# Two stacked transformer models on one core: what each block does to hand its result to the next one

## The chip, the cores and the metric

The kernel runs on one core of a Trainium2 chip. The metric is the device time of one execution in microseconds (us), lower is better. All arithmetic is float32; matrix products of weights and activations are done as three products of reduced float32 parts, explained below.

## The reference, cut to what matters

256 tokens of width 1024 go through two models one after the other. The first has two equal layers; each computes a modulated root-mean-square norm of the running sum `x`, a mixer (sparse and compressed attention of two kinds), and adds a gated, normalized result. The second has four sublayers: neighbourhood attention, a gated feed-forward net, latent attention, and a mixture of eight experts.

```python
# first model, per layer l
h = rmsnorm(x, g_pre[l]) * (1.0 + scale) + shift
y = hybrid_mixer(h, ...)
x = x + gate * rmsnorm(y, g_post[l])
# second model, per sublayer; rmsnorm without a weight
h = _rmsnorm(x) * (1 + sc[:, None, :]) + sh[:, None, :]
m = attention(h)            # or feed-forward, or experts
x = x + g[:, None, :] * m
```

`scale`, `shift` and `gate` come from products of one conditioning vector with large matrices (here called "ada" sums); they don't depend on `x`. What matters here is the seam between two of these blocks: nothing of the next block's products can begin before its `h` is there, `h` needs the mean square of a whole row of `x`, and `x` needs the whole last product of the block before.

## The kernel before, in words

**Layout.** `x` is held as two halves of 128 token rows (m = 0 and m = 1) with 1024 columns each. The products need features on the partitions, so `h` is kept turned, in 8 tiles of 128 features by 256 tokens (`hb`, and its two parts `h_hi` and `h_lo`). Every float32 operand is split into a high part (ScalarE, ACT, copies it with rounding) and a low part (VectorE, DVE, subtracts), and one product is three matmuls (`mm3`, L831 to L835): hi*hi, hi*lo, lo*hi.

**Weights.** All weights come as steps of 128x2048 elements (1 MB) through a ring of 6 raw buffers, loaded by SyncE's queue (L681) as soon as a buffer is free. For a weight step ACT writes `w_hi` (`hi_to`, L1625) and DVE writes `w_lo` (`raw_to`/`split_to`, L2217) into a ring of 3 split buffers; TensorE (PE) frees a split buffer with `split_used`. For an "ada" step DVE does eight scaled sums (L2233, L2235) instead. A projection slot of PE is two weight steps, kh = 0 and kh = 1; kh = 0 uses feature tiles 0 to 3, kh = 1 tiles 4 to 7. There are 48 matmuls of 256 columns in one half slot of `feat_pieces` (L869).

**Order.** Each engine has one queue, written out by hand and executed in order; semaphores tie them. Phases are `lay0`, `lay1`, `na`, `ffn`, `mla` and then routing and experts.

**A seam (lay0 to lay1 as the example).** PE's last product `out_moba(1)` (L1038) ends. ACT squares and sums the output rows (L1960), GpSimd (POOL) turns the sum into 1/rms in two instructions, the mean (L734) and the power (L739), DVE scales the output by the gate (L2728) and adds it to `x` (L2731), for m = 0 early and for m = 1 last. Then `squares` (L1633): ACT squares all of `x`, m = 0 and m = 1; POOL `rstd` (L729) makes both 1/rms at once; meanwhile DVE makes `w_lo` of the next block's first weight step and the per-feature factors `ab` (`make_ab`, L2291); then `normed` (L2253) writes `xn` = x/rms, both halves, and only then PE turns it: `turn` (L913) does 16 transposes, four for each of four PSUM banks (a bank holds two feature tiles of 256 tokens), and signals `turned` after each bank. ACT and DVE scale and shift the turned tiles (`scaled`, banks 0 and 2 on DVE, 1 and 3 on ACT), ACT writes `h_hi`, DVE `h_lo` (`lo` in `norm`, L2261), each signal `h` meaning one pair of feature tiles. DVE's order is scaled(0), lo(0), scaled(2), lo(1), lo(2), lo(3). PE's first slot waits for `h` 2 before kh = 0 and for `h` 4 before kh = 1; in `ffn` PE waits for `h` 4 before everything. After `norm` DVE goes on to `w_lo` of the second weight step (in lay1 it first multiplies gate and g_post, L2521, 1.23 us).

In the feed-forward block `x` is updated by `update_x` (L2306) after the last product of both row halves, in eight DVE instructions of 512 columns (L2313, L2314); PE's last work there is the 24 matmuls of `down(10)` over both row halves, then `ada(11)`. In `na` the update is L2800 and L2802, in `ffn` and `na` without a second norm. POOL also fills `nakz` with zeros in `na` (L760 and L762), waiting for `xn` and for `turned`.

```python
            def turn(src):
                for b in range(4):
                    for k in range(2):
                        for m in range(MT):
                            ...
                    last.then_inc(*e.inc("turned"))
```

Of the kernel before, what the change touches and what calls it, by code (L numbers as in the profile page):

```python
# [12 lines left out]
P = 128  # L13
# [152 lines left out]
def ring_plan(size, lengths):  # L166
# [78 lines left out]
    "dve": {"pre": 26, "lay0": 93, "lay1": 81, "na": 46, "ffn": 104, "mla": 29, "rt": 10, "go": 23, "moe0": 11, "moeA": 7, "moeB": 7, "moeZ": 7, "more": 7},  # L245
# [47 lines left out]
    "rstd": {"lay": 3, "na": 1, "ffn": 1, "mla": 3, "rt": 2, "end": 1},  # L293
# [6 lines left out]
    "sq": {"lay": 4, "na": 2, "ffn": 2, "mla": 6, "rt": 2, "end": 2},  # L300
# [9 lines left out]
    "x_half": {"mla": 1},  # L310
# [82 lines left out]
def build(nc, dram):  # L393
    ctx = ExitStack()
    with ctx:
# [326 lines left out]
        def _(pool):  # L722
# [6 lines left out]
            def rstd(sq_wait, spans):  # L729

                pool.wait_ge(*e.at("sq", sq_wait))
                pool.sem_inc(settled)
                for a, b, n in spans:
                    g.tensor_scalar(st[:, s_ms + a:s_ms + b], st[:, s_sq + a:s_sq + b],  # L734
                                    1.0 / n, EPS, ALU.mult, ALU.add).then_inc(*e.inc("mean_sq"))
                    pool.wait_ge(*e.last("mean_sq"))
                    pool.sem_inc(settled)
                a, b = spans[0][0], spans[-1][1]
                g.tensor_tensor(st[:, s_rs + a:s_rs + b], st[:, s_ms + a:s_ms + b],  # L739
                                st[:, s_half:s_half + b - a], ALU.pow).then_inc(*e.inc("rstd"))  # L740
# [10 lines left out]
            for l in range(2):  # L751
                e.enter(f"lay{l}")
                rstd(2, [(0, 2, D)])
                rstd(3, [(2, 3, D)])
                rstd(4, [(3, 4, D)])
            e.enter("na")
            rstd(2, [(0, 2, D)])
# [69 lines left out]
        def _(pe):  # L827
# [22 lines left out]
            def tok_pieces(n, banks, width, first=True, fresh=False):  # L850

                for kh in range(2):
                    w = arrived(n + kh)
                    if fresh:
                        pe.wait_ge(*e.at("h", 2 * kh + 2))
                    for m in range(MT):
                        if kh == 0 and first:
                            bank_free(banks[m])
                        for k in range(4):
                            kt = kh * 4 + k  # L860
                            lhs = [a[:, kt, m * P:(m + 1) * P] for a in (hh, hl)]
                            rhs = [a[:, k * width:(k + 1) * width] for a in w]
                            last = mm3(PS[:, banks[m], 0:width], lhs, rhs, kt == 0, kt == KT - 1)
                            if m == MT - 1 and k == 3:
                                last.then_inc(*e.inc("split_used"))
                            if k % 2 == 1:
                                yield

            def feat_pieces(n, banks, order=(0, 1, 2, 3), fresh=False):  # L869

                for kh in range(2):
                    w = arrived(n + kh)
                    if fresh:
                        pe.wait_ge(*e.at("h", 2 * kh + 2))
                    for i, f in enumerate(order):
                        b = banks[i // 2]
                        if kh == 0 and i % 2 == 0:
                            bank_free(b)
                        for k in range(4):
                            kt = kh * 4 + k  # L880
# [2342 lines left out]
```

## Time and profile before

| what | value |
|---|---|
| median of 3 runs | 1628.31 us (1627.68 to 1629.74) |
| the profiled execution, its own time | 1633.32 us |
| its span in the trace | 1631.4 us |
| PE / DVE / ACT / POOL busy | 87% / 75% / 53% / 4% |
| DMA, mean over the span | 247 GB/s |
| mean granted TensorE clock | 0.94 |

The page's parts are: busy time of each engine over the span, the same in 40 slices with the granted clock, DMA queues, the chain that ended last, the costliest groups by line. The timeline lists instructions by start time and length, with the engine's idle time before one, and what ended it, in brackets. A row with "x2" is several merged neighbours: start of the first, busy time of all.

### The profile page before, as it was taken

What the parts mean: (1) busy time and instruction counts of PE and PEld (TensorE: products, weight loads), DVE (VectorE), ACT (ScalarE), POOL (GpSimd) and SP (SyncE); (2) the same over time, 40 slices, a digit from 0 to 9 for tenths busy, and PEclk for the clock granted to TensorE, in tenths of its full rate; (3) what the DMA queues carried; (4) which work ended last, traced back from release to release, by engine and by line L of the source; (5) the groups of instructions that cost most, each with busy time, mean ns of one, the idle gap of its engine ahead of it and who ended that gap; (6) DMA issues with size and microseconds to landing.
All of it is one profiled execution on the core that took longest, in us unless ns stands there. A gap on an engine that the chain in (4) does not pass through costs nothing.

```text
span 1631.4 us, 21240 instructions
## 1 busy us (share of the span) xinstructions
PE 1414.9 (87%) x7628; PEld 1188.4 (73%) x7628; DVE 1216.6 (75%) x1484; ACT 861.2 (53%) x1210; POOL 65.3 (4%) x82
## 2 busy tenths in 40 slices
PE   2999878899979896899985896999999999999992
PEld 2878668787668775898964785877777777777772
DVE  7978646776485647788767535889889889899895
ACT  2434444345344534334414645677777777777772
POOL 1000000000010000000001004000000000000001
PEclk9989998899889998999987996999999999999996
DMA  9945415555165724677753214889999999999782
GB/s 398 369 173 212 173 60 197 197 209 203 52 237 217 269 78 154 253 276 290 297 201 125 102 61 153 315 335 364 355 349 355 338 353 364 342 366 362 281 361 90
DMA packets 61537, 403.08 MB, mean 247 GB/s; under 512 B 6534, under 2 KB 9734, under 8 KB 15116
## 3 DMA queue, kind: packets, MB, share of 16 engines
q1 hardware_dynamic: 52416, 379.45, 61.4%
q10 hardware_dynamic: 7020, 15.17, 2.6%
q0 software_dynamic: 2016, 7.34, 1.2%
q8 instruction: 52, 0.85, 0.2%
q14 instruction: 33, 0.27, 0.0%
HBM read 393.01 MB, written 8.91 MB: 246 GB/s over the span
## 4 chain that ended last, share of the span: by engine, by line
PE 49%; DVE 33%; ACT 10%; issue 4%; DMA 3%; POOL 1%; ACTq 0%; DVEq 0%; SPq 0%; POOLq 0%
DVE w_lo L2217 18%; PE PS L833 13%; PE PS L835 12%; PE PS L834 12%; DVE acc L2235 4%; ACT w_hi L1625 4%; DMA raw<-in_ws 2%; ACT xg L1720 2%; PE PS L986 1%; PE PS L903 1%; PE PS L1006 1%; DVE a_lo L2384 1%; PE PS L995 1%; DVE hb L2393 1%; DVE hb L2395 1%
## 5 line engine op out<-in xcount | busy, mean ns | idle before, releaser
L2217 DVE TENSOR_TENSOR w_lo<-raw,w_hi 128x2048 fp32r<-128x2048 f32 x287 | 659.6, 2298 | 150.7 <-ACT w_hi L1625 127.9
L1625 ACT ACTIVATE w_hi<-raw 128x2048 fp32r<-128x2048 f32 x287 | 548.0, 1919 | 246.0 <-PE PS L835 221.9
L833 PE MATMUL PS<-w_hi,h_hi 128*128 128x512 f32 (+2 forms) x812 | 337.3, 415 | 26.2 <-DVE h_lo L2660 8.3
L835 PE MATMUL PS<-w_hi,h_lo 128*128 128x512 f32 (+2 forms) x812 | 320.1, 394 | 0.0
L834 PE MATMUL PS<-w_lo,h_hi 128*128 128x512 f32 (+2 forms) x812 | 319.5, 393 | 0.0
L833 PE MATMUL PS<-h_hi,w_hi 128*128 128x256 f32 x776 | 234.5, 302 | 33.4 <-DVE h_lo L2268 14.4
L834 PE MATMUL PS<-h_lo,w_hi 128*128 128x256 f32 x776 | 226.8, 292 | 0.0
L835 PE MATMUL PS<-h_hi,w_lo 128*128 128x256 f32 x776 | 226.6, 292 | 0.0
L833 PEld LDWEIGHTS PS<-w_hi,h_hi 128*128 128x128 f32 x812 | 156.8, 193 | 74.4 <-DVE w_lo L2217 16.0
L2235 DVE SCALAR_TENSOR_TENSOR acc<-raw,cs,acc 128x512 f32<-128x512 f32 x252 | 189.5, 752 | 9.0
L833 PEld LDWEIGHTS PS<-h_hi,w_hi 128*128 128x128 f32 x776 | 156.2, 201 | 38.5 <-issue 11.6
L835 PEld LDWEIGHTS PS<-w_hi,h_lo 128*128 128x128 f32 x812 | 156.2, 192 | 33.1
L834 PEld LDWEIGHTS PS<-w_lo,h_hi 128*128 128x128 f32 x812 | 157.1, 193 | 29.0 <-issue 2.2
L834 PEld LDWEIGHTS PS<-h_lo,w_hi 128*128 128x128 f32 x776 | 156.2, 201 | 2.4 <-issue 1.7
L835 PEld LDWEIGHTS PS<-h_hi,w_lo 128*128 128x128 f32 x776 | 155.9, 201 | 0.0
L833 PE MATMUL PS<-w_hi,a_hi 128*128 128x512 f32 x340 | 140.0, 412 | 17.3 <-DVE a_lo L2384 11.1
L835 PE MATMUL PS<-w_hi,a_lo 128*128 128x512 f32 x340 | 134.4, 395 | 0.0
L834 PE MATMUL PS<-w_lo,a_hi 128*128 128x512 f32 x340 | 133.7, 393 | 0.0
L1886 ACT ACTIVATE lgp<-lgp,st 128x128 f32<-128x128 f32 (+1 forms) x96 | 42.9, 449 | 123.9 <-DVE st L2536 123.9
L833 PEld LDWEIGHTS PS<-w_hi,a_hi 128*128 128x128 f32 x340 | 64.4, 190 | 37.6 <-DVE w_lo L2217 23.1
L835 PEld LDWEIGHTS PS<-w_hi,a_lo 128*128 128x128 f32 x340 | 64.4, 189 | 14.6
L834 PEld LDWEIGHTS PS<-w_lo,a_hi 128*128 128x128 f32 x340 | 64.6, 190 | 11.9
(310 smaller groups left out, 1397.9 us busy)
## 6 DMA issues: line engine op xcount, KB each, us to landing
raw<-in_ws SPq DMA_DIRECT2D x359, 1024.0 KB, 5.5
y_rows<-ysb ACTq DMA_DIRECT2D x10, 512.0 KB, 7.2
rp<-in_rp ACTq DMA_DIRECT2D x8, 384.0 KB, 4.8
ckb<-in_ck ACTq DMA_DIRECT2D x2, 1024.0 KB, 6.5
y_rows<-ones ACTq DMA_DIRECT2D x3, 512.0 KB, 8.2
x<-in_x SPq DMA_DIRECT2D x1, 1024.0 KB, 13.4
gpost<-in_gpost ACTq DMA_DIRECT2D x2, 512.0 KB, 5.7
x_rows<-xn_f ACTq DMA_DIRECT2D x2, 512.0 KB, 3.8
```

Of the source, the lines that this page charges most:

```text
L833: t.matmul(out, lhs[0], rhs[0], start=start, stop=False, skip_group_check=True)
L834: t.matmul(out, lhs[0], rhs[1], start=False, stop=False, skip_group_check=True)
L835: return t.matmul(out, lhs[1], rhs[0], start=False, stop=stop, skip_group_check=True)
L903: last = t.matmul(PS[:, 3, c:c + 1], a[:, c * P:(c + 1) * P], ones[:, 0:1], start=True, stop=True)
L986: t.matmul(PS[:, PS_S[i % 2], 0:2 * u["nk"]].rearrange("p (a k) -> p a k", a=2), u["q"], u["k"], start=True, stop=True).then_inc(*e.inc("s ...
L995: last = t.transpose(PS[:, PS_PT, c * P:(c + 1) * P], lgp[:, i % 3, c * P:(c + 1) * P], ident)
L1006: last = t.matmul(PS[:, PS_O, h * HD:(h + 1) * HD], ptp[:, i % 2, (a * n + c) * P:(a * n + c + 1) * P], u["v"][a][c], start=c == 0, stop=c ...
L1625: a.activation(wh[:, SPL_AT[e.phase][i], :], raw[:, r, :], ACT.Copy).then_inc(*e.inc("hi"))
L1720: ins = a.activation(xg[:, kt, :], PS[:, 6 + kt // 4, (kt % 4) * P:(kt % 4 + 1) * P], ACT.Identity, scale=ab[:, 0, kt:kt + 1], bias=ab[:, ...
L1886: a.activation(part, part, ACT.Exp, bias=mn(c), scale=-1.0, accum_out=sm(c)).then_inc(*e.inc("probs"))
L2217: v.tensor_tensor(wl[:, s, :], raw[:, r, :], wh[:, s, :].bitcast(F32), ALU.subtract).then_inc(*e.inc("raw_used"))
L2235: ins = v.scalar_tensor_tensor(out=dst, in0=w, scalar=c[:, kt:kt + 1], in1=dst, op0=ALU.mult, op1=ALU.add)
```

## The change

At each of the four seams lay0 to lay1, lay1 to na, na to ffn and ffn to mla, the first 128 rows go ahead. As soon as x of m = 0 is updated, ACT squares it (after `w_hi` of the next block's first step), POOL makes its 1/rms, DVE makes `w_lo` of that step and writes xn of m = 0 (`hand_on`), and PE transposes it (8 transposes, or 4 in mla, where two banks are still in use) before xn of m = 1 is there. For m = 1 the squares are taken in two halves of 512 columns, each with its own sum; POOL takes the mean of the first sum, and adds the second with one more instruction. x of m = 1 is updated by column halves. After xn of m = 1 PE needs 2 transposes for a bank, instead of 4.

DVE's order in `norm` becomes scaled(0), lo(0), lo(1), scaled(2), lo(2), lo(3), and the first slot of a block runs over feature tiles 0 and 1, then 2 and 3 (and 4 and 5, then 6 and 7), waiting for one `h` more each time; in ffn the wait for `h` 4 goes. In lay0 (no seam ahead of it) POOL's work and the waits are split in the same way, and the order of `norm` and of the first slot changes too. In ffn the last down product does the m = 0 rows first, then `ada(11)`, then m = 1 by column halves. ACT makes `w_hi` of the third step after `h_hi`, and not before it.

```diff
+            def rstd_halves(col, other, sums, done, name):
+                pool.wait_ge(*e.at(sums, 2))
+                pool.sem_inc(settled)
+                mean(col, col + 1, D, name)
+                pool.wait_ge(*e.at(sums, 3))
+                pool.sem_inc(settled)
+                g.tensor_scalar(st[:, s_ms + other:s_ms + other + 1], st[:, s_sq + other:s_sq + other + 1],
+                                1.0 / D, st[:, s_ms + col:s_ms + col + 1], ALU.mult,
+                                ALU.add).then_inc(*e.inc(name))
+                ...
+                g.tensor_tensor(... ALU.pow).then_inc(*e.inc(done))
...
+            for block, following in (("lay0", "lay1"), ("lay1", "na")):
+                e.resume(block)
+                rstd(1, [(2, 3, D)])
+                e.enter(following)
+                rstd(1, [(0, 1, D)], "sq_x", "rstd_x", "mean_x")
+                e.resume(block)
+                rstd_halves(3, 7, "sq", "rstd", "mean_sq")
+                e.resume(following)
+                rstd_halves(1, 6, "sq_x", "rstd_x", "mean_x")
...
             def feat_pieces(n, banks, order=(0, 1, 2, 3), fresh=False):
                 for kh in range(2):
                     w = arrived(n + kh)
-                    if fresh:
-                        pe.wait_ge(*e.at("h", 2 * kh + 2))
-                    for i, f in enumerate(order):
+                    for ks in ((0, 1), (2, 3)) if fresh else ((0, 1, 2, 3),):
+                        if fresh:
+                            pe.wait_ge(*e.at("h", 2 * kh + ks[-1] // 2 + 1))
+                        for i, f in enumerate(order):
...
+            def turn(src, banks_free=4):
+                ...
+                pe.wait_ge(*e.at("xn", 1))
+                for b in range(banks_free):
+                    part(b, 0)
+                pe.wait_ge(*e.at("xn", 2))
                 for b in range(4):
+                    if b >= banks_free:
+                        part(b, 0)
+                    part(b, 1).then_inc(*e.inc("turned"))
...
+                    order = ([(k, m, c) for k in range(2) for m in range(MT) for c in range(2)] if not ends else
+                             [(k, 0, c) for k in range(2) for c in range(2)] +
+                             [(k, 1, c) for c in range(2) for k in range(2)])
+                        if ends and (k, m, c) == (1, 0, 1):
+                            last.then_inc(*e.inc("out_m0"))
+                            ada(FFN_SLOTS)
...
-            pe.wait_ge(*e.at("h", 4))
             ffn()
...
+            def squares_on(xn):
+                for half in range(2):
+                    square(xn, 1, half)
+                hi_to(2)
...
+                following, xn = (("lay1", xn_l), ("na", xn_n))[l]
+                start(following)
+                square(xn, 0)
+                e.resume(f"lay{l}")
+                for c, col in enumerate((3, 7)):
+                    act.wait_ge(*e.at("split_used", 19 + c))
+                    a.activation(xn_l[:, 1, c * 512:(c + 1) * 512], PS[:, PS_OUT[1] + c, :], ACT.Square, ...)
...
+            def hand_on(following, xn):
+                block = e.phase
+                start(following)
+                split_to(1)
+                normed(xn, 0)
+                e.resume(block)
...
                 scaled(0)
                 lo(0)
+                lo(1)
                 scaled(2)
-                lo(1)
                 lo(2)
                 lo(3)
...
+                hand_on(*(("lay1", xn_l), ("na", xn_n))[l])
+                for c in range(2):
+                    dve.wait_ge(*e.at("split_used", 19 + c))
+                    dve.wait_ge(*e.at("sq", 2 + c))
+                    link(v.tensor_tensor(scaled_y[:, 1, halves[c]], PS[:, PS_OUT[1] + c, :], gate[0][:, halves[c]], ...))
+                dve.wait_ge(*e.at("rstd", 2))
+                for c, name in enumerate(("x_half", "x")):
+                    v.scalar_tensor_tensor(out=x[:, 1, halves[c]], ...).then_inc(*e.inc(name))
...
+            update_first(4, gate[0])
+            hand_on("mla", xn_m)
+            dve.wait_ge(*e.at("out_half", 1))
+            update_half(4, 0, gate[0])
+            dve.wait_ge(*e.at("split_used", SPLITS["ffn"]))
+            update_half(4, 1, gate[0])
```

## Rows read from the trace of the kernel before

**Rows 1.** The page, part 1: busy time of the engines, share of the span.

```profile
PE 1414.9 (87%) x7628; PEld 1188.4 (73%) x7628; DVE 1216.6 (75%) x1484; ACT 861.2 (53%) x1210; POOL 65.3 (4%) x82
```

**Rows 2.** Timeline at the seam lay0 to lay1, DVE: start, length, line, operation [idle before].

```profile
234.13 1.28 DVE L2731 SCALAR_TENSOR_TENSOR x<-scaled_y,st,x 128x1024 f32<-128x1024 f32 x1
...
240.86 1.28 DVE L2731 SCALAR_TENSOR_TENSOR x<-scaled_y,st,x 128x1024 f32<-128x1024 f32 x1
...
242.18 2.29 DVE L2217 TENSOR_TENSOR w_lo<-raw,w_hi 128x2048 fp32r<-128x2048 f32 x1
...
245.51 1.54 DVE L2257 TENSOR_SCALAR xn_l<-x,st 128x1024 f32<-128x1024 f32 x2 [0.38 <-POOL st L739]
...
250.82 0.69 DVE L2268 TENSOR_TENSOR h_lo<-hb,h_hi 128x512 fp32r<-128x512 f32 x1 [1.36 <-ACT h_hi L1658]
...
252.70 0.69 DVE L2268 TENSOR_TENSOR h_lo<-hb,h_hi 128x512 fp32r<-128x512 f32 x1
...
258.25 4.62 DVE L2217 TENSOR_TENSOR w_lo<-raw,w_hi 128x2048 fp32r<-128x2048 f32 x2
```

**Rows 3.** Timeline of the same seam, ACT and POOL.

```profile
240.04 0.55 POOL L739 TENSOR_TENSOR st<-st 128x1 f32<-128x1 f32 x1 [0.18 <-POOL st L734]
...
242.21 1.04 ACT L1639 ACTIVATE xn_l<-x 128x1024 f32<-128x1024 f32 x1
...
243.54 0.99 POOL L734 TENSOR_SCALAR st<-st 128x2 f32<-128x2 f32 x1 [2.95 <-ACT xn_l L1639]
...
249.18 1.02 ACT L1654 ACTIVATE hb<-PS,ab 128x256 f32<-128x256 f32 x2 [2.23 <-PE PS L920]
```

**Rows 4.** Timeline of the same seam, PE, and the ACT instruction that waits for kh = 0.

```profile
247.11 3.68 PE L920 MATMUL PS<-par,xn_l 128*128 128x128 f32 x16 [8.79 <-DVE xn_l L2257]
...
253.54 0.36 PE L833 MATMUL PS<-h_hi,w_hi 128*128 128x256 f32 x1 [2.76 <-DVE h_lo L2268]
...
261.11 1.92 ACT L1625 ACTIVATE w_hi<-raw 128x2048 fp32r<-128x2048 f32 x1 [5.17 <-PE PS L835]
```

**Rows 5.** Windows: busy us of PE, PEld, DVE, ACT, POOL, then granted clock, DMA.

```profile
254.00:257.60 3.60, 3.60 (x21) 3.60 (x20) 2.01 (x3) 1.95 (x4) 0.00 (x0) 0.54 0.81 289
257.60:262.00 4.40, 4.40 (x38) 4.40 (x38) 4.33 (x3) 0.89 (x1) 0.00 (x0) 0.98 0.20 24
```

**Rows 6.** Timeline at the seam lay1 to na: POOL's second memset, PE's first product.

```profile
462.06 1.80 POOL L762 MEMSET nakz<- 128x2048 f32 x1 [1.93 <-PE PS L920]
...
464.76 0.47 PE L833 MATMUL PS<-w_hi,h_hi 128*128 128x512 f32 x1 [2.76 <-DVE h_lo L2268]
```

**Rows 7.** Timeline at the seam na to ffn: x of either half, w_hi, PE.

```profile
612.13 1.92 ACT L1625 ACTIVATE w_hi<-raw 128x2048 fp32r<-128x2048 f32 x1 [0.85 <-PE PS L835]
...
613.37 1.22 DVE L2802 TENSOR_TENSOR x<-x,scaled_y 128x1024 f32<-128x1024 f32 x1
...
619.24 1.23 DVE L2802 TENSOR_TENSOR x<-x,scaled_y 128x1024 f32<-128x1024 f32 x1
...
634.92 0.58 PE L833 MATMUL PS<-h_hi,w_hi 128*128 128x256 f32 x1 [5.82 <-DVE h_lo L2268]
...
657.21 0.58 PE L833 MATMUL PS<-h_hi,w_hi 128*128 128x256 f32 x1 [5.41 <-DVE hb L2334]
```

**Rows 8.** Timeline at the seam ffn to mla: first and last of eight update instructions, PE.

```profile
854.93 0.69 DVE L2313 TENSOR_TENSOR scaled_y<-PS,gate 128x512 f32<-128x512 f32 x1 [11.74 <-PE PS L835]
...
860.01 0.69 DVE L2314 TENSOR_TENSOR x<-x,scaled_y 128x512 f32<-128x512 f32 x1
...
872.09 0.64 PE L833 MATMUL PS<-w_hi,h_hi 128*128 128x416 f32 x1 [2.99 <-DVE h_lo L2268]
```

**Rows 9.** Timeline of lay0's start: DVE's last h_lo of kh = 0, PE, DVE's first later idle time.

```profile
40.36 0.69 DVE L2268 TENSOR_TENSOR h_lo<-hb,h_hi 128x512 fp32r<-128x512 f32 x1
...
41.20 0.55 PE L833 MATMUL PS<-h_hi,w_hi 128*128 128x256 f32 x1 [5.84 <-DVE h_lo L2268]
...
84.50 0.29 DVE L2536 CUSTOM_DVE_ANT_0 lgp<-lc,PS 128x128 f32<-128x128 f32 x1 [0.22 <-DVE vsw L2683]
```

More of the change, by code:

```diff
@@ L244 @@
     "downs_done": {"end": 1},
-    "dve": {"pre": 26, "lay0": 93, "lay1": 81, "na": 46, "ffn": 104, "mla": 29, "rt": 10, "go": 23, "moe0": 11, "moeA": 7, "moeB": 7, "moeZ": 7, "more": 7},
+    "dve": {"pre": 26, "lay0": 94, "lay1": 82, "na": 47, "ffn": 101, "mla": 29, "rt": 10, "go": 23, "moe0": 11, "moeA": 7, "moeB": 7, "moeZ": 7, "more": 7},
     "dve_end": {"end": 21},
@@ L263 @@
     "mc": {"mla": 1},
-    "mean_sq": {"lay": 3, "na": 1, "ffn": 1, "mla": 5, "rt": 2, "end": 1},
+    "mean_sq": {"lay": 3, "mla": 4, "rt": 2, "end": 1},
+    "mean_x": {"lay0": 2, "lay1": 3, "na": 3, "ffn": 3, "mla": 3},
     "o_used": {"lay": 6, "na": 4, "mla": 4},
-    "out_m0": {"lay": 1, "na": 1, "mla": 1},
+    "out_half": {"ffn": 1},
+    "out_m0": {"lay": 1, "na": 1, "ffn": 1, "mla": 1},
     "over": {"go": 1},
@@ L292 @@
     "rp_in3": {"na": 2},
-    "rstd": {"lay": 3, "na": 1, "ffn": 1, "mla": 3, "rt": 2, "end": 1},
+    "rstd": {"lay": 2, "mla": 2, "rt": 2, "end": 1},
+    "rstd_x": {"lay": 2, "na": 2, "ffn": 2, "mla": 2},
     "rwb": {"mla": 1},
@@ L299 @@
     "split_used": {"pre": 3, "lay": 20, "na": 16, "ffn": 33, "mla": 9, "moe0": 21, "moeA": 21, "moeB": 21, "moeZ": 21, "more": 21},
-    "sq": {"lay": 4, "na": 2, "ffn": 2, "mla": 6, "rt": 2, "end": 2},
+    "sq": {"lay": 3, "mla": 4, "rt": 2, "end": 2},
+    "sq_x": {"lay0": 2, "lay1": 3, "na": 3, "ffn": 3, "mla": 3},
     "stored": {"end": 2},
@@ L309 @@
     "x_f": {"go": 2, "moe0": 2, "moeA": 2, "moeB": 2, "moeZ": 2, "more": 2},
-    "x_half": {"mla": 1},
+    "x_half": {"lay": 1, "na": 1, "ffn": 1, "mla": 1},
     "x_hi": {"go": 2, "moe0": 2, "moeA": 2, "moeB": 2, "moeZ": 2, "more": 2},
@@ L750, in _ @@
             pool.wait_ge(*e.at("consts", 2))
[L751 to L757, printed above, removed]
+            e.enter("lay0")
+            for m in range(MT):
+                rstd(m + 1, [(m, m + 1, D)], "sq_x", "rstd_x", "mean_x")
+            for block, following in (("lay0", "lay1"), ("lay1", "na")):
[7 more added lines that the diff above has]
+                rstd_halves(1, 6, "sq_x", "rstd_x", "mean_x")
             pool.wait_ge(*e.at("xn", 2))
@@ L1711, in ffn @@
                 ada_out(FFN_SLOTS - 1, 2)
+                start("mla")
+                square(xn_m, 0)
+                e.resume("ffn")
                 ada_out(FFN_SLOTS, 2)
@@ L1805, in _ @@
             e.enter("lay0")
-            squares(xn_l, ahead=False)
+            for m in range(MT):
+                square(xn_l, m)
             act.wait_ge(*e.at("y", 0))
@@ L1823, in layer @@
                 if l == 1:
-                    start("lay1")
-                    squares(xn_l)
+                    e.resume("lay1")
+                    squares_on(xn_l)
                     act.wait_ge(*e.at("y", 0))
@@ L2052, in _ @@
             start("ffn")
-            squares(xn_f)
+            square(xn_f, 0)
+            squares_on(xn_f)
             get_brow(4)
@@ L2058, in latent @@
             def latent():
-                start("mla")
-                squares(xn_m)
+                e.resume("mla")
+                squares_on(xn_m)
                 act.dma_start(mc[:], dram["mc"]).then_inc(*e.inc("mc", 16))
@@ L2500, in _ @@
             e.enter("lay0")
-            normed(xn_l)
+            for m in range(MT):
+                normed(xn_l, m)
             e.resume("pre")
@@ L2509, in layer @@
                 else:
-                    start("lay1")
+                    e.resume("lay1")
                 split_to(1)
```

272 lines of the change are left out of this document (135 added, 137 removed).

## The prediction, written before the run

> **What bounds the kernel now.** I read the page's busy times first: PE works 87% of the span, DVE 75% [rows 1], so time can be had where PE stands idle and at the places where DVE is the engine that ends last. Then the timeline of each engine around one seam [rows 2 to 4]. The reader is to see a chain that passes through all engines one at a time while PE waits: x of m = 1 is done at 242.14 (240.86 + 1.28), ACT squares it by 243.35, POOL needs until 245.40, both xn take until 247.05, 16 transposes until 250.8, scaling and splitting until 253.39, and at 253.54 PE starts [rows 2 to 4]. PE is idle 8.79 + 2.76 us of it [rows 4]. The other three seams have the same chain; ffn adds 5.82 us ahead of its first product, since it waits for all of h [rows 7]. At last I looked at what holds the next stage after it has begun, since only that tells what an early start is worth.
>
> **One seam, step by step (lay0 to lay1).**
> (1) *What goes ahead.* x of m = 0 is done at 235.41 [rows 2]. Its square takes 1.04 plus about 0.15 for the sum: 236.6. DVE goes from x to w_lo of the new block: 235.45 to 237.74 (2.29 [rows 2]). POOL's mean took 0.99 for two numbers while such a w_lo ran, and ended at 244.53, 0.06 after w_lo (242.18 + 2.29) [rows 2, 3]. So I let POOL wait here too: mean at 237.8, power 0.18 later for 0.55 [rows 3], 238.5; xn of m = 0, half of 1.54 [rows 2], 238.6 to 239.35. Its 8 transposes (3.68 / 16 = 0.23 each [rows 4]) fill idle PE until 241.2.
> The Trainium skill, page "SBUF — State Buffer" (on the shared port pair), says that DVE and GpSimd share one pair of ports as an exclusive lock, which a DVE instruction with two SBUF inputs holds against a GpSimd instruction that reads SBUF; the trace agrees, with the 0.99 just named. Without that rule xn of m = 0 would come about 1.0 earlier, and the sum below would be some 1 to 2 us larger over all seams.
> (2) *What it delays.* x of m = 1 stands behind all this in DVE's queue. Two gate products of 512 columns at 0.69 + 0.03 (the same shape in [rows 8]) end at 240.8; the power for y is ready by 240.6; the two x updates at about 0.75 each end at 242.4, against 242.14: 0.3 late.
> (3) *x of m = 1 to xn.* Before, 247.05 - 242.14 = 4.91. After: square of the second half 0.62 (half of 1.04, plus 0.1) and its sum 0.1, POOL start 0.2, add 0.19 (not under a w_lo now; bounds 0.19 and 0.99), 0.18, power 0.55 [rows 3], 0.1, one xn 0.77: 2.75 with the handover ahead. PE starts to turn at 245.2 and not at 247.11: 1.9 earlier.
> (4) *Turn to h.* ACT's scaled(1) began 2.07 after the turn's start (249.18 - 247.11 [rows 3, 4]); 4 transposes are left ahead of it instead of 8, which is 0.92 less. That carries lo(0) (250.82 to 251.51, so 4.40 after the turn before, 3.48 after). PE may now start behind lo(0): 3.63 after the turn, against 6.43 (253.54 - 247.11). h 2 follows with lo(1) 0.73 later, at 4.21, against 6.28 (253.39), since scaled(2) (1.12 of DVE) no longer stands between. So PE's first product comes 1.9 + 2.8 = 4.7 earlier, and everything of DVE behind h 2 (lo(2), lo(3), w_lo) 1.9 + 2.05 = 3.95 earlier.
> (5) *What is late next.* PE ran kh = 0 from 253.54 to about 261.0 (ACT's w_hi waits for its end, 261.11 [rows 4]) and then needs the second w_lo, ready at 258.25 + 2.3 = 260.55. After, these are 256.3 and 256.6, so w_lo is now the last: **4.3 gained**. From there on w_hi waits for PE and DVE for w_hi, so the gain stays.
>
> **The other places.**
> *lay1 to na*: the same chain, first product at 464.76 [rows 6]; there is no gate product on DVE, so w_lo is early and PE's own start counts: **4.7**. One thing could take from it: POOL's second memset of nakz (1.80, 462.06 to 463.86 [rows 6]) now begins before lo(0), where before it began just behind its start. Bounds: 0, and 1.2 if lo(0) had to wait for its end. No row shows a DVE subtraction inside a memset; the nearest, the memset itself, kept its 1.80 over DVE's work, so I take 0. The same section of the Trainium skill's page would give 0 too, since a memset reads no SBUF; no run here shows it so far.
> *na to ffn*: x of m = 0 is done at 614.6, of m = 1 at 620.47 [rows 7]. After: w_lo to 616.9, POOL to 617.7, xn to 618.55, then four half updates at 0.72 to 621.5: 1.0 late, and the turn starts 1.9 + 0.3 - 1.0 = 1.1 earlier. The turn before began as far behind x as in lay (4.96), at 625.43, and 9.49 passed from there to PE's first product [rows 7]. Now PE starts at 634.92 - 1.1 - (9.49 - 3.63) = 627.9, 7.0 earlier; but DVE's chain only 1.1 + 2.05 = **3.2**. What counts is the second stall at 657.21, where PE has waited 5.41 for DVE's hb to free a PSUM bank [rows 7]; DVE works without a gap from h 4 to there. So 3.2, and PE's stall there grows to some 9.
> *ffn to mla*: before, eight updates run from 854.93 to 860.70 [rows 8], ahead of them 24 matmuls. After, m = 0 is ready 12 matmuls earlier and x of m = 1 at about 861.3, 0.6 late; the turn 1.5 earlier. mla turns only two banks early, but scaled(1) needs just those. First product 4.3 earlier; DVE's next chain (tables for the router, then the rotated keys) 3.6. What ends last there mixes both: **3.9**. The ada(11) put between the two row halves only changes places.
> *lay0's start*: h 2 comes from lo(1), 40.36 + 0.69 = 41.05 [rows 9], and without scaled(2) ahead of it at 39.9: 1.15 earlier; PE starts 1.9 earlier. DVE has no idle time from there to 84.5 [rows 9], PE waits for it at the end: **1.2**.
> The third w_hi behind h_hi costs nothing: its w_lo comes 2.3 later still. SyncE's loads follow raw_used, which only moves forward; ACT's DMAs (gpost, rp, brow, mc) stay at the same place behind the squares and are covered by POOL and the transposes.
>
> **Sum.** 4.3 + 4.7 + 3.2 + 3.9 + 1.2 = 17.3. Against it stands PE's clock. After a pause PE ran 21 matmuls in 3.60 us at a granted 0.54, which is the level of 1.2 GHz for nearly all of it, and then 38 in 4.40 at 0.98 (2.4 GHz) [rows 5]: 0.171 against 0.116 each. kh = 0 with 48 took 7.5 us instead of 5.6: a restart costs 1.9. This cost stands in the times above, and I keep it. The pauses become shorter but are cut in two, and the second stall of ffn grows. Bounds: from 6 more such costs (11.4) to two fewer (-3.8). I take one more, **2.0**, for ffn, where the pause clearly grows. 17.3 - 2.0 = 15.3. The profiled execution took 1633.32 (span 1631.4 and 1.9 around it): 1618.0. The median of the runs shown lies 5.0 below it, so I forecast **1613.0 us**.
>
> **Rivals.**
> *A, the clock takes most of it* (0.20). For it: 1.2 GHz in the products after the pause [rows 5]; each cut pause may bring a slow stretch of its own. Against: the pauses get shorter in all, and where w_lo or DVE is the last, a slow kh = 0 is hidden. Price: 4 to 6 more restarts at 1.9: gain 6 to 10, 1618 to 1622.
> *B, given back in the next stage* (0.05). If the weight loads or a DVE chain sets the pace of each block whenever it starts, an early start is a longer stall. Against: w_hi waits for PE after the first step in lay1 [rows 4]. Gain under 3: 1625 to 1628.
> *C, slower* (0.04). One mechanism: the hand-on stands in DVE's queue ahead of x of m = 1 and itself needs ACT's w_hi, for which a split buffer must be free. If that came free only with the block's last product (238.3, which is 247.11 less 8.79 [rows 4]), w_hi would end at 240.2, w_lo at 242.5, xn of m = 0 at 243.5 and x of m = 1 at about 246.6 instead of 242.14. At 4.4 late it takes all of the 4.3; from there on a seam loses: some 1629 to 1635. Against: the same w_hi began at 612.13, well before DVE could take the last product at 618.0 (619.24 less the gate product of 1.23) [rows 7], and in the lay phases its buffer belonged to step 17, used long before.
> *D, more than forecast* (0.09). The starts fall so that PE is at 2.4 GHz earlier, and DVE's delays of step 2 are smaller: gain 19 to 23, 1605 to 1609.
> *My forecast* (0.62): gain 10 to 19, 1609 to 1618.
>
> **How the numbers follow.** 0.2% is 3.3 us, about what a measurement of this kernel tells from no change. Faster: forecast, A and D whole, and a little of B: 0.92. Same: most of B and the near end of C: 0.04. Slower: the rest of C and what I have not seen: 0.04. The range from 1606.5 to 1621.5 holds the forecast, half of D and most of A, about 0.85.
>
> **What would show it.** x of m = 1 done 0.3 (lay), 1.0 (ffn), 0.6 (mla) late; POOL's mean of m = 0 near 1 us long and ending with w_lo; 8 transposes alone in the pause; PE's first product about 3.6 us behind the second group of transposes, against 6.4 (9.5 in ffn). In lay1 PE waits for w_lo between kh = 0 and kh = 1. In ffn a stall of about 9 us ahead of the second slot. If the lead at the first product is there and is gone at the end of the block, B is right; if the leads are there and PE's matmuls of 256 columns are long at more places, A; if x of m = 1 is 4 us late, C.

## The result, and the profile after

The changed kernel takes 1639.3 us (median of 6 runs, 1634.7 to 1643.2) where the kernel before took 1628.9 beside it (6 runs, 1627.7 to 1631.2): ratio 1.0057, 95% interval 1.0040 to 1.0074. It is slower by some 9 us; forecast were 1613.0 and a gain of 15.3. The profiled execution took 1643.2, its span is 1641.4.

The page's busy times of after, as in [rows 1], are nearly the same: PE has 8.9 us more for the same number of matmuls, POOL 16 small instructions more.

```profile
PE 1423.8 (87%) x7628; PEld 1191.2 (73%) x7628; DVE 1216.9 (74%) x1488; ACT 863.4 (53%) x1222; POOL 72.0 (4%) x98
```

The seam lay0 to lay1, on DVE in the timeline of after (start, length, line, operation, idle before): compare with [rows 2].

```profile
244.05 1.28 DVE L2799 SCALAR_TENSOR_TENSOR x<-scaled_y,st,x 128x1024 f32<-128x1024 f32 x1
245.37 2.29 DVE L2283 TENSOR_TENSOR w_lo<-raw,w_hi 128x2048 fp32r<-128x2048 f32 x1
248.54 0.75 DVE L2322 TENSOR_SCALAR xn_l<-x,st 128x1024 f32<-128x1024 f32 x1 [0.88 <-POOL st L734]
249.33 1.42 DVE L2807 TENSOR_TENSOR scaled_y<-PS,gate 128x512 f32<-128x512 f32 x2
250.78 1.54 DVE L2811 SCALAR_TENSOR_TENSOR x<-scaled_y,st,x 128x512 f32<-128x512 f32 x2
254.39 0.75 DVE L2322 TENSOR_SCALAR xn_l<-x,st 128x1024 f32<-128x1024 f32 x1 [1.46 <-POOL st L763]
...
264.32 4.62 DVE L2283 TENSOR_TENSOR w_lo<-raw,w_hi 128x2048 fp32r<-128x2048 f32 x2
```

The same seam on POOL, as in [rows 3]: the mean for m = 0 under w_lo, and the two sums and the power for m = 1.

```profile
246.71 1.00 POOL L738 TENSOR_SCALAR st<-st 128x1 f32<-128x1 f32 x1 [2.95 <-ACT xn_l L1685]
...
252.49 0.19 POOL L738 TENSOR_SCALAR st<-st 128x1 f32<-128x1 f32 x1 [2.30 <-ACT xn_l L1685]
253.29 0.27 POOL L758 TENSOR_SCALAR st<-st 128x1 f32<-128x1 f32 x1 [0.62 <-ACT xn_l L1685]
253.75 0.54 POOL L763 TENSOR_TENSOR st<-st 128x1 f32<-128x1 f32 x1 [0.18 <-POOL st L758]
```

PE, from the last step of lay0's output product on. That step in the timeline of before:

```profile
232.58 0.50 PE L833 MATMUL PS<-w_hi,h_hi 128*128 128x512 f32 x1 [1.48 <-DVE h_lo L2660]
```

The same step in after, and what follows; for the later rows see [rows 4, 6, 7, 8].

```profile
242.50 0.50 PE L862 MATMUL PS<-w_hi,h_hi 128*128 128x512 f32 x1 [1.48 <-DVE h_lo L2732]
...
249.35 1.09 PE L954 MATMUL PS<-par,xn_l 128*128 128x128 f32 x8 [1.10 <-DVE xn_l L2322]
255.20 1.97 PE L954 MATMUL PS<-par,xn_l 128*128 128x128 f32 x8 [4.76 <-DVE xn_l L2322]
258.89 0.55 PE L862 MATMUL PS<-h_hi,w_hi 128*128 128x256 f32 x1 [1.72 <-DVE h_lo L2341]
...
478.23 0.76 PE L862 MATMUL PS<-w_hi,h_hi 128*128 128x512 f32 x1 [1.73 <-DVE h_lo L2341]
...
643.88 0.55 PE L862 MATMUL PS<-h_hi,w_hi 128*128 128x256 f32 x1 [1.73 <-DVE h_lo L2341]
...
670.15 0.58 PE L862 MATMUL PS<-h_hi,w_hi 128*128 128x256 f32 x1 [8.46 <-DVE hb L2405]
...
881.56 0.68 PE L862 MATMUL PS<-w_hi,h_hi 128*128 128x416 f32 x1 [0.87 <-DVE h_lo L2341]
```

The seams do what was forecast. From the last step of the output product to lay1's first product it took 253.54 - 232.58 = 20.96 us before, and 258.89 - 242.50 = 16.39 now. But the whole seam begins 9.9 us later than before (242.50 against 232.58). PE's timeline shows where that lag arises: at lay0's attention, two rows with an idle time that the kernel before doesn't have. Two more follow in lay1, and a short one in na.

```profile
156.07 0.47 PE L862 MATMUL PS<-w_hi,h_hi 128*128 128x512 f32 x1 [2.02 <-ACT kmz L1927]
...
181.05 0.76 PE L862 MATMUL PS<-w_hi,h_hi 128*128 128x512 f32 x1 [5.61 <-ACT vm L1904]
...
373.81 0.70 PE L862 MATMUL PS<-w_hi,h_hi 128*128 128x512 f32 x1 [1.71 <-ACT kmz L1927]
...
400.00 0.77 PE L862 MATMUL PS<-w_hi,h_hi 128*128 128x512 f32 x1 [5.26 <-ACT vm L1904]
...
557.64 0.47 PE L862 MATMUL PS<-w_hi,h_hi 128*128 128x512 f32 x1 [1.38 <-ACT nakz L2054]
```

L862 is a product, and its releaser is a copy of a finished slot's rows out of a PSUM bank. What frees a bank for a product is `bank_free`, and the diff does move that. In `tok_pieces` of the kernel before the wait is inside the loop over m, right before m's own products (the edit of e2 below shows these lines); now it stands in a loop of its own ahead of both:

```python
                    for m in range(MT):
                        if kh == 0 and first:
                            bank_free(banks[m])
                    # then the products, for m = 0 and m = 1
```

A slot of two banks so waits for the second bank before it computes into the first. Slot 7 of a layer uses banks 2 and 0, slot 6 banks 0 and 1 (`LAY_BANK`), and the second bank of each is the first one of the slot before, whose copy stands behind other work in ACT's queue. The section on the change quotes `feat_pieces`, where the wait for a bank stays in place, and not this function.

### The profile page after: what moved, and what is told of

Same layout as the page of the kernel before. It is cut to its first block, busy times and chain, and to the rows that moved or that the text cites. A ratio compares the mean times of both kernels' runs of the same rounds, so it can differ in the third digit from the quotient of the medians.

```text
span 1641.4 us, 21304 instructions
## 1 busy us (share of the span) xinstructions
PE 1423.8 (87%) x7628; PEld 1191.2 (73%) x7628; DVE 1216.9 (74%) x1488; ACT 863.4 (53%) x1222; POOL 72.0 (4%) x98
## 4 chain that ended last, share of the span: by engine, by line
PE 46%; DVE 35%; ACT 10%; issue 4%; DMA 3%; POOL 1%; DVEq 0%; ACTq 0%; SPq 0%; POOLq 0%
DVE w_lo L2283 19%; PE PS L862 12%; PE PS L864 12%; PE PS L863 12%; DVE acc L2301 5%; ACT w_hi L1670 3%; DMA raw<-in_ws 2%; ACT xg L1780 2%; PE PS L1029 1%; PE PS L937 1%; DVE a_lo L2455 1%; DVE hb L2464 1%; DVE hb L2466 1%; DVE h_lo L2421 1%; PE PS L1339 1%
## 5 line engine op out<-in xcount | busy, mean ns | idle before, releaser
L862 PE MATMUL PS<-w_hi,h_hi 128*128 128x512 f32 (+2 forms) x812 | 339.3, 418 | 38.0 <-ACT vm L1904 10.9
L862 PE MATMUL PS<-h_hi,w_hi 128*128 128x256 f32 x776 | 234.6, 302 | 31.0 <-DVE hb L2405 8.5
L862 PEld LDWEIGHTS PS<-w_hi,h_hi 128*128 128x128 f32 x812 | 157.6, 194 | 89.7 <-issue 27.7
L862 PEld LDWEIGHTS PS<-h_hi,w_hi 128*128 128x128 f32 x776 | 156.4, 202 | 36.3 <-issue 10.8
L862 PE MATMUL PS<-w_hi,a_hi 128*128 128x512 f32 x340 | 140.3, 413 | 17.3 <-DVE a_lo L2455 11.1
L862 PEld LDWEIGHTS PS<-w_hi,a_hi 128*128 128x128 f32 x340 | 64.4, 190 | 38.1 <-DVE w_lo L2283 23.1
L864 PEld LDWEIGHTS PS<-w_hi,a_lo 128*128 128x128 f32 x340 | 64.4, 189 | 14.7
## 6 DMA issues: line engine op xcount, KB each, us to landing
x<-in_x SPq DMA_DIRECT2D x1, 1024.0 KB, 13.3
```

Source lines behind the costliest of these rows:

```text
L862: t.matmul(out, lhs[0], rhs[0], start=start, stop=False, skip_group_check=True)
L864: return t.matmul(out, lhs[1], rhs[0], start=False, stop=stop, skip_group_check=True)
```

## The experiments

Eight kernels, each timed five or six times beside the kernel before. Its median was 1630.8 beside the first four and 1629.7 beside the other four; ratios are to that.

**e1_own_bank**: the changed kernel, with each bank's wait back ahead of its own products.

```diff
-                    for m in range(MT):
-                        if kh == 0 and first:
-                            bank_free(banks[m])
                     for ks in ((0, 1), (2, 3)) if fresh else ((0, 1, 2, 3),):
                         ...
                         for m in range(MT):
+                            if kh == 0 and ks[0] == 0 and first:
+                                bank_free(banks[m])
```

> The changed kernel, but in token slots each bank is waited for right ahead of its own products again, as before. Theory 1 (the change asks for both PSUM banks of a token slot ahead of its first product, so PE waits in lay0 and lay1 for ScalarE to empty bank 0 and bank 1): the idle time of 5.6 and 2.0 us ahead of slots 7 and 6 goes, with what follows from it, which by the traces is some 22 us; the seams keep their gains: about 1616 us, 12 to 13 below before. Theory 2 (TensorE's clock after cut pauses, the rival A of the prediction, grown to the whole loss): the two waits are harmless, since attention sets the pace there, and the time stays at 1633 to 1643 us.

Measured: 1612.4 us (1607.8 to 1616.7), ratio 0.9896 (0.9874 to 0.9918). The five waits are gone from its timeline. This one edit decides the sign of the whole change: with it undone the change gains 16.9 us (1.04% of 1628.3), where the forecast was 15.3.

**e2_before_hoist**: the kernel before, with both waits ahead of the products in every token slot, by one line, and nothing else.

```diff
                     for m in range(MT):
                         if kh == 0 and first:
                             bank_free(banks[m])
+                    for m in range(MT):
                         for k in range(4):
```

**e3_before_hoist7**: the same, for slot 7 of each layer only.

```diff
                     w = arrived(n + kh)
                     ...
+                    both = n == 14 and e.phase in KIND
+                    if both and kh == 0:
+                        for m in range(MT):
+                            bank_free(banks[m])
                     for m in range(MT):
-                        if kh == 0 and first:
+                        if kh == 0 and first and not both:
                             bank_free(banks[m])
```

> The kernel before, with the two bank waits of a token slot put ahead of its first product and nothing else. Theory 1: slower than before by 20 to 25 us, 1649 to 1654 us. Theory 2: within 3 us of before.

> The kernel before, with the two bank waits put together only in slot 7 of the two layers (banks 2 and 0; bank 0 is still held by the slot just ahead, whose rows ScalarE copies to vm). Theory 1 with slot 7 as the main place (idle 5.6 against 2.0 us): 13 to 18 us slower than before, two thirds or more of what the kernel with all waits together loses. If slots 6 and 7 share alike: about half. Theory 2: no change.

Measured: e2 1654.0 us, ratio 1.0129 (1.0105 to 1.0152); e3 1644.3, ratio 1.0085 (1.0064 to 1.0105). In e2's timeline the five waits stand at the same products as in after's, 16.3 us of idle time in all. The edit alone costs 1.29%, 21 us, slot 7 alone 13.8 us. Now the question is why, since PE is idle only 5.32 + 5.26 us more in e3. Windows show it: busy us of PE, PEld, DVE, ACT, POOL, then granted clock, DMA share, GB/s. First before: its stretch at the place of the pause, then from the product that follows ACT's `qm` in lay0 to lay1's first product, then lay1 whole.

```profile
174.96:180.11 5.15, 5.15 (x26) 3.32 (x24) 4.44 (x10) 1.44 (x5) 0.00 (x0) 1.00 0.64 229
140.10:253.54 113.44, 94.89 (x500) 76.63 (x501) 70.41 (x128) 55.58 (x117) 3.17 (x6) 0.92 0.39 141
253.54:464.76 211.22, 184.53 (x1075) 156.95 (x1075) 138.85 (x250) 93.08 (x195) 6.75 (x8) 0.91 0.47 172
```

The same of e3, the first row being what follows the pause.

```profile
179.23:183.93 4.70, 4.70 (x16) 4.07 (x17) 0.00 (x0) 0.34 (x1) 0.00 (x0) 0.56 0.36 145
138.47:260.95 122.48, 99.98 (x500) 80.06 (x501) 70.36 (x128) 55.54 (x117) 3.17 (x6) 0.87 0.35 131
260.95:479.35 218.40, 187.01 (x1074) 158.88 (x1075) 138.81 (x250) 93.17 (x195) 6.75 (x8) 0.90 0.44 166
```

In lay0 the stretch is 9.0 us longer; PE has the same 500 matmuls and is busy with them 99.98 - 94.89 = 5.1 us longer, at a clock of 0.87 instead of 0.92. Behind the pause it worked at a granted 0.56, its level of 1.2 GHz for nearly all of it; the same place ran at 1.00 before. So the pause is paid for twice over, once as idle time and once as slow matmuls. How much the second part is can be read by following the same products through both timelines: across the pause in lay0 e3 falls back by 7.5 us (it is 1.6 ahead of before in front of it and 5.8 behind after it), of which 5.3 are idle; across the one in lay1 again by 7.3 (from 7.4 to 14.7). Two times 7.4 is 14.8, and the times gave 13.8 (10.4 to 17.1).

The changed kernel against e1 shows the same bill. After, from the same two points:

```profile
137.72:258.89 121.17, 99.86 (x500) 79.27 (x501) 68.98 (x128) 54.43 (x120) 4.26 (x10) 0.90 0.36 132
258.89:478.23 219.34, 189.80 (x1075) 160.33 (x1075) 139.18 (x253) 94.17 (x198) 7.73 (x12) 0.90 0.45 166
```

And e1:

```profile
137.25:244.80 107.55, 94.42 (x500) 75.32 (x501) 68.99 (x128) 54.14 (x120) 4.26 (x10) 0.94 0.40 149
244.80:450.23 205.43, 181.93 (x1075) 155.34 (x1075) 139.19 (x253) 93.64 (x198) 7.73 (x12) 0.93 0.47 177
```

13.6 us in lay0 and 13.9 in lay1: 5.4 + 7.9 = 13.3 of the 27.5 are longer busy time for the same matmuls, 14.2 idle time (the four waits of the two layers are 14.6, the rest evens out). Of the 27.5, 26.2 arise between the start of a wait and the place where the clock is back: 2.3 and 8.2 in lay0, 3.3 and 12.4 in lay1, always slot 6 first. By the ratios after and e1 are 26 us apart; the two executions shown differ by more, 35.4, as after's is the slowest of its six and e1's the fastest, and 3.1 of the rest stand in na, with the fifth wait, 3.7 behind mla's first product, where neither has such a wait. Against before, PE's busy time in the two stages of after is 10.2 longer, and not 13.3.

Slot 7's wait of some 5.3 us costs 7.3 to 7.5 in e3, where no wait of slot 6 stands ahead of it, and more where one does: 8.2 and 12.4 here, 11.3 and 12.4 in e2 against before. In lay1 the first 10 us behind the wait ran so in e3:

```profile
397.42:407.42 10.00, 10.00 (x36) 7.33 (x37) 0.59 (x4) 2.27 (x8) 0.00 (x0) 0.78 0.14 57
```

And in after, where the clock stayed at 0.50 until 414.5:

```profile
400.00:410.00 10.00, 10.00 (x22) 6.16 (x23) 0.59 (x4) 1.22 (x5) 0.00 (x0) 0.50 0.14 58
```

That the earlier wait is the reason fits all four places, the 8.2 only just; each is one execution, and no run isolates it.

**e4_no_first_pair**: e1 without the start on the first pair: DVE's order in `norm` as before, kh = 0 waits for two `h` and ffn for four. The first line stands in the token slots, in the feature slots and in mla.

```diff
-                    for ks in ((0, 1), (2, 3)) if fresh else ((0, 1, 2, 3),):
+                    for ks in ((0, 1, 2, 3),):
...
+            pe.wait_ge(*e.at("h", 4))
             ffn()
...
                 lo(0)
-                lo(1)
                 scaled(2)
+                lo(1)
```

> The kernel with the banks' own waits, and without the early first pair of turned features: PE waits for h 2 and h 4 as before (h 4 in ffn), DVE's order in the norm is as before. The early m = 0 rows and the column halves stay. By the steps of the prediction the first product comes 2.8 us later again and DVE's w_lo 1.1 later: over lay0's start, lay1, na, ffn and mla the loss against the kernel with own waits is 1.2 + 1.4 + 2.8 + 1.2 + 1.5, some 8 us; so about 1624 us. If the starts of PE counted for nothing: 0 to 2 us.

Measured: 1620.1 us, ratio 0.9937 (0.9915 to 0.9958), 0.41% (6.7 us) behind e1, where some 8 were expected; the two intervals only just touch. PE's first product of lay1 now stands 5.57 behind the second group of transposes, not 3.69; it is 1.9 later and not 2.8, since the 0.92 of the early transposes stays in e4:

```profile
244.23 1.97 PE L952 MATMUL PS<-par,xn_l 128*128 128x128 f32 x8 [4.76 <-DVE xn_l L2321]
249.80 0.55 PE L862 MATMUL PS<-h_hi,w_hi 128*128 128x256 f32 x1 [3.61 <-DVE h_lo L2340]
```

So, as far as times with such intervals tell, some 40% of e1's gain comes from the first pair (6.7 of 16.9), and the rest from all else in the change: the rows of m = 0 that go ahead, and m = 1 by halves.

**e6_turn_late**: e1, but PE transposes nothing before both xn are there.

```diff
-                pe.wait_ge(*e.at("xn", 1))
+                pe.wait_ge(*e.at("xn", 2))
                 for b in range(banks_free):
                     part(b, 0)
```

> As e1_own_bank, but PE transposes nothing before xn of both row halves is there (xn of m = 0 is still written early). Theory of the prediction (4 transposes ahead of the bank that scaled(1) needs, and not 8, are worth 0.92 us a seam): first product 0.9 to 1.0 later behind the turn at four seams, 3.7 us in all, about 1616. Rival 1 (ACT and DVE have other work then, so the early transposes bring nothing): 1612. Rival 2 (16 transposes in one go after a longer pause also run at the low clock): 1618 to 1620.

Measured: 1622.5 us, ratio 0.9948 (0.9929 to 0.9967), 0.52% behind e1. My 0.92 a seam was wrong for this kernel: its loop does all 8 transposes of m = 0 first, so here the whole of them (8 x 0.23 = 1.84), not 4, is put ahead of the first bank. The trace has 5.40 from turn to product in lay1, na and ffn where e1 has 3.69, 1.71 a seam. In mla, where the loop does only 4 ahead, it has 4.55 (856.52 to 861.07) against 3.69, 0.86, which is the price that I had given to 4. Together 6.0. The 8.5 us of the times are more, but their intervals leave room for 6.

```profile
244.65 3.68 PE L952 MATMUL PS<-par,xn_l 128*128 128x128 f32 x16 [6.97 <-DVE xn_l L2320]
...
250.05 0.55 PE L862 MATMUL PS<-h_hi,w_hi 128*128 128x256 f32 x1 [1.72 <-DVE h_lo L2339]
```

**e7_ffn_h4**: e1, but ffn waits for all of h before its first product.

```diff
+                pe.wait_ge(*e.at("h", 4))
                 for s in range(FFN_SLOTS):
```

> As e1_own_bank, but in ffn PE waits for all of h ahead of its first product, as the kernel before did. Theory of the prediction (in ffn only DVE's chain counts, the early first product turns into a longer stall ahead of the second slot): PE's first product some 3 us later, the stall of 8.46 us shorter by as much and ending at the same time, 0 in all: 1612, within 1. Rival (the early start is worth its time): 3 us more, 1615 to 1616. A second rival (one pause fewer at the low clock): 1610.

Measured: 1615.2 us, ratio 0.9899 (0.9878 to 0.9920), 0.03% from e1. Times with such intervals don't tell 0 from the rival's 3 us; the trace of this stage does. e7:

```profile
613.81 1.97 PE L952 MATMUL PS<-par,xn_f 128*128 128x128 f32 x8 [4.64 <-DVE xn_f L2321]
...
621.48 0.58 PE L862 MATMUL PS<-h_hi,w_hi 128*128 128x256 f32 x1 [5.70 <-DVE h_lo L2340]
...
643.76 0.58 PE L862 MATMUL PS<-h_hi,w_hi 128*128 128x256 f32 x1 [5.56 <-DVE hb L2404]
```

In after the first product stands 3.70 behind the turn and the second slot 29.97 (640.18, 643.88, 670.15), in e1 3.69 and 29.94; here 7.67 and 29.95. Of the 4.0 us that PE starts earlier without this wait, 2.9 are given back as a longer stall and 1.1 by a first slot that takes longer (17.8 us from its first product to the stall, against 16.7 in e7). The early first product of ffn is worth nothing, in this stage: the stall ends at the same distance from the turn.

**e8_wlo_late**: e1, with w_lo of the next block's first step behind x of m = 1, not ahead of xn of m = 0.

```diff
                 start(following)
-                split_to(1)
                 normed(xn, 0)
...
                 if e.phase != "lay0":
+                    split_to(1)
                     normed(xn, 1)
```

> As e1_own_bank, but w_lo of the next block's first weight step stands behind x of m = 1 in DVE's queue (as in the kernel before) and not between x of m = 0 and xn of m = 0. Theory (POOL's instructions that read SBUF wait for the end of w_lo): POOL's mean for m = 0 takes 0.19 and not 1.00, x of m = 1 comes 0.5 to 1.0 earlier, but POOL's second sum for m = 1 now ends with w_lo, so xn of m = 1 is 0.9 to 1.4 later: some 4 us slower than e1_own_bank, 1616 to 1617. Rival (POOL isn't held by w_lo; the 1.00 has another cause): x of m = 1 earlier and xn of m = 1 with it, 2 to 3 us faster than e1_own_bank, 1609 to 1610.

Measured: 1616.9 us, ratio 0.9913 (0.9896 to 0.9931). The interval overlaps e1's, so the time alone doesn't decide; the rows do. POOL in e8:

```profile
233.01 0.19 POOL L738 TENSOR_SCALAR st<-st 128x1 f32<-128x1 f32 x1 [2.95 <-ACT xn_l L1683]
...
239.09 2.11 POOL L758 TENSOR_SCALAR st<-st 128x1 f32<-128x1 f32 x1 [0.62 <-ACT xn_l L1683]
```

And DVE's w_lo in e8, which ends at 241.06, as that POOL instruction does (241.20):

```profile
238.77 2.29 DVE L2281 TENSOR_TENSOR w_lo<-raw,w_hi 128x2048 fp32r<-128x2048 f32 x1
```

Free of w_lo, the mean takes 0.19; the sum that now meets it takes 2.11, where it takes 0.27 otherwise. The rival, that POOL isn't held, is out. DVE's rows also show both sides of the trade: from the start of x of m = 0 (230.35 in e8, 229.95 in e1) to the end of x of m = 1 it takes 7.77 instead of 8.28, to xn of m = 1 11.68 instead of 10.35, so 0.5 us are won and 1.3 lost.

**e5_fill**: e1, with DVE's work for the first half of m = 1 put into the 0.88 us in which DVE waited for POOL.

```diff
-            def hand_on(following, xn):
+            def hand_on(following, xn, between):
                 block = e.phase
                 start(following)
                 split_to(1)
+                e.resume(block)
+                between()          # layers: the gate product of half 0; na, ffn: update_half(.., 0, ..)
+                e.resume(following)
                 normed(xn, 0)
```

> As e1_own_bank (every bank waited for at its own first product), and DVE's work for column half 0 of m = 1 (layers: the gate product; na and ffn: gate product and addition) is put between w_lo and xn of m = 0, where DVE stood idle 0.88 us at every seam, since POOL's mean had waited for w_lo. Theory (the idle time was DVE's own chain, so work that doesn't depend on POOL fills it): x of m = 1 comes 0.55 earlier in the layers and 0.7 to 0.9 earlier in na and ffn, PE's first product as well, some 2.5 to 3 us in all: about 1609 to 1610 where e1_own_bank had 1612.4. Rival (POOL's second sum and power hold x of m = 1 anyway, or xn of m = 0 gets late for PE): 0, 1612.

Measured: 1609.8 us (1607.6 to 1610.8), ratio 0.9876 (0.9857 to 0.9894): the fastest kernel here, 20 us (1.24%) below before. Against e1 the 0.2% isn't told apart by the times. In its trace, on DVE, the idle time is down to 0.16, and from the end of w_lo to xn of m = 1 it takes 6.23 (240.09 - 233.86) where e1 takes 6.74 (240.30 - 233.56). Of the 0.72 us of idle time that are filled 0.51 are kept; x of m = 1 now waits 0.25 for POOL's power, so the rival has a small part in it:

```profile
231.57 2.29 DVE L2281 TENSOR_TENSOR w_lo<-raw,w_hi 128x2048 fp32r<-128x2048 f32 x1
233.89 0.69 DVE L2808 TENSOR_TENSOR scaled_y<-PS,gate 128x512 f32<-128x512 f32 x1
234.75 0.75 DVE L2320 TENSOR_SCALAR xn_l<-x,st 128x1024 f32<-128x1024 f32 x1 [0.16 <-POOL st L734]
...
240.09 0.75 DVE L2320 TENSOR_SCALAR xn_l<-x,st 128x1024 f32<-128x1024 f32 x1 [1.46 <-POOL st L763]
```

## Why the prediction was wrong

**The step that failed is one that the prediction doesn't have.** It costs the seams and says of all else that it "costs nothing" or stays; the new place of the waits in `tok_pieces` got no term. I had read that function's change as one of the order in which feature tiles are taken. By e2 this edit costs 21 us alone, by the ratios of e1 and after 26 in the changed kernel, more than all seams gain. Two rows of the timelines of PE and ACT in before would have given its size for slot 7 of lay0: its first product, and ACT's copy of slot 6's rows, whose first half frees bank 0 at 180.15 + 0.54 = 180.7, 5.4 us later. Before, only the products of m = 1, from 181.96 on, had to wait for it, and it was free by then.

```profile
175.31 0.48 PE L833 MATMUL PS<-w_hi,h_hi 128*128 128x512 f32 x1
...
180.15 1.07 ACT L1843 ACTIVATE vm<-PS 128x512 f32<-128x512 f32 x2
```

No rival covers it either: C is a seam that loses, with 4.4 us late on x of m = 1, and that did not happen.

Why is bank 0 free so late? The timeline of ACT in after: the copy `vm` stands in ACT's queue behind the exponentials of an attention step, those wait for DVE's `lgp`, and DVE is in a w_lo of 2.29 (175.87 to 178.16) before it. That this is why it is late is read from the rows, no run takes a link out. PE waits for the end of this chain and has nothing else to do in its queue.

```profile
178.85 0.51 ACT L1947 ACTIVATE lgp<-lgp,st 128x256 f32<-128x256 f32 x1 [5.84 <-DVE st L2608]
...
180.33 1.07 ACT L1904 ACTIVATE vm<-PS 128x512 f32<-128x512 f32 x2
```

**Steps (1) to (4) held, mostly within 0.2 us.** The two that miss by 0.5 are the length of ffn's stall and mla's first product. All in after:

| | forecast | measured |
|---|---|---|
| POOL's mean of m = 0 | about 1, ends with w_lo | 1.00, ends 247.71, w_lo 247.66 |
| x of m = 1 late, lay / ffn / mla | 0.3 / 1.0 / 0.6 | 0.26 / 0.98 / 0.7 |
| turn to first product | 3.63 | 3.69, 3.70 in ffn and mla |
| first product of lay1 earlier | 4.7 | 20.96 - 16.39 = 4.57 |
| first product of na earlier | 4.7 | 18.0 - 13.5 = 4.5 |
| DVE's chain in lay1 earlier (its w_lo) | 3.95 | 9.92 - 6.07 = 3.85 |
| first product of ffn earlier | 7.0 | 15.9 - 9.0 = 6.9 |
| second stall of ffn | about 9, ending 3.2 earlier | 8.46, ending 15.9 - 12.9 = 3.0 earlier |
| first product of mla earlier | 4.3 | 13.3 - 9.5 = 3.8 |

(The lags: at lay0's last step 9.92, at DVE's w_lo 264.32 - 258.25 = 6.07; ahead of ffn, at the last h_lo of na, 627.24 - 611.38 = 15.9, at ffn's first product 643.88 - 634.92 = 9.0, at the stall 12.9; at lay1's last output step 461.77 - 443.76 = 18.0, at na's first product 13.5; late in ffn 13.3, at mla's first product 9.5. The x of m = 1 in lay ended 9.82 behind lay0's last output step, against 9.56 before; in ffn 6.86 against 5.88 behind x of m = 0 [rows 7]; in mla 4.73 behind the last product, or 6.75 with the 2.02 us of `ada(11)` that now stand ahead of it, against 6.04. The three x ends are read from DVE's timelines of after, at 252.32, 637.31 and 874.99.)

**Step (5), what is late next,** held in ffn: e7 takes 4.0 us of PE's earlier start away and the end doesn't move. In lay1 it was wrong in the detail: PE was to wait for the second w_lo, and it didn't. Its first half slot took 8.36 us (258.89 to 267.25) and not 7.5, as the clock stood at 0.50 for its first 5.7 us, so it ended 0.6 behind w_lo (264.32 + 2.31), and the gain was 9.92 - 6.40 = 3.5 instead of 4.3. e4 is the counterpart for the order on DVE. That the gain stays holds by e1: at the ends of its stages it keeps its lead over before (PE's first product 14.5 ahead in na, 22.2 in mla), so rival B, given back in the next stage, is out; B had some right in ffn only, where it was in the sum.

**POOL and the lock.** [rows 3] gave 0.99 under a w_lo; after gave 1.00, e8 0.19 and 2.11. The rule that I cited of the Trainium skill, page "SBUF — State Buffer", on the shared port pair, is thereby shown here both ways: take w_lo away, and the mean is short; put it over another instruction, and this one is long. The memset in na costs nothing, as taken: it ran its 1.80 us beside DVE, whose h_lo subtraction at 477.39, two SBUF inputs, lay inside it and kept its length (two of them took 1.42, as in ffn without a memset), so that half of the rule agrees too. The first product there stands 3.70 behind the turn, as at the other seams:

```profile
476.56 1.80 POOL L791 MEMSET nakz<- 128x2048 f32 x1 [0.22 <-PE PS L954]
```

**The clock.** Against the gain I set 2.0 us, from 1.9 for one restart [rows 5]. Inside the seams it can't be told from noise: e1's 16.9 stands beside 17.3 without and 15.3 with the term, its interval reaches from 13.3 to 20.5. But the size per restart was right where it counted: the pause in e3 made its next six products start 0.43 us apart instead of 0.23, and 5.32 of idle time became 7.5 us of lag by the time the clock was back (174.96 against 173.32 ahead of it, 180.11 against 185.94 behind). Only 2.15 of lay0's 5.1 us of longer busy time are there, right behind the pause. Another 2.1 lie in a stretch that begins 20 us later, at 0.87 against 0.99 in the matching one of before. Before:

```profile
198.00:224.00 26.00, 23.01 (x127) 18.16 (x125) 13.27 (x31) 13.12 (x31) 0.00 (x0) 0.99 0.14 43
```

The same stretch of e3:

```profile
204.00:230.00 26.00, 25.09 (x123) 19.23 (x122) 11.77 (x29) 13.12 (x31) 0.00 (x0) 0.87 0.11 41
```

It would be wrong to charge this to the pause. The matching stretch of lay1 ran at 0.87 in before itself, without any such wait ahead of it:

```profile
407.25:433.25 26.00, 24.83 (x124) 18.97 (x122) 11.48 (x28) 13.12 (x31) 0.00 (x0) 0.87 0.12 41
```

In after, behind the longest slow stretch of all, it ran at 1.00 (428.79 to 454.79), and e6, which has no wait in lay0, at 0.87 there (195.81 to 221.81). This stretch goes fast or slow from one execution or layer to the next, and 2 us of a stage come and go with it.

Behind a seam the clock cost a little more than I had taken: in lay1 PE worked for 5.7 us at 0.50 in after and for 4.8 in e1, against 4.1 at 0.60 in before.

**What stays open.** By its two parts, e2's loss and e1's gain, the change should cost 21 - 17 = 4 us, and it costs 9. The intervals of e1 and e2 reach 3.6 and 3.8 us to either side and that of after 2.8, so this may be chance, or the two parts add up to more than each alone; no run was made to tell. The traces speak for chance: over the same two stages e2 is 26.1 us longer than before, and after 27.5 longer than e1, nearly the same price in either kernel; in na it is 1.5 and 3.1.

## What to carry to other kernels

In a diff of an engine with one queue, list every wait that changes its place, also where the line only leaves a loop, and ask for each what stood between it and its old place: all of that now waits too. Price such a wait by the end of the releaser on its own engine, not by the engine that it stands on, and, where PE is the bound, add the slow matmuls behind it: here a pause of 5.3 us cost 7.4 alone, and 8.2 to 12.4 where another had gone ahead.

When an engine waits for POOL, look first whether DVE's long instructions with two SBUF inputs hold it, and fill DVE's idle time with work that doesn't depend on POOL (e5).

## What the runs showed of the hardware

The idle time of PE is not its price. Single waits of 5.3 us put PE 7.3 to 7.5 us back, since the matmuls behind them ran at a granted 0.53 to 0.56 (mostly the 1.2 GHz level). In the two layers four waits of 14.6 us in all made 27.5 us between two executions, 13.3 of it as longer busy time for the same matmuls, the most of it right behind the waits, in lay1 with 14.5 us at 0.50. A low clock far from a pause proves little: the same stretch of code ran at 0.87 and at 1.00 in different executions and layers, with and without a pause ahead.

And a DVE subtraction of 2.29 us with two SBUF inputs held a POOL instruction of 0.27 for 2.11 and one of 0.19 for 1.00, each to its own end, while a POOL memset beside a DVE subtraction kept its 1.80. So what such a POOL instruction costs is set by how much of a DVE instruction of this kind is left when it comes.
